# Memory output end, its norm and the first four query tiles in groups of 256 tokens

## The reference, cut to what matters

```
o = jnp.einsum('bhqm,bmhd->bqhd', p, v).reshape(bsz, seq, D_MODEL)
mem_out = o @ w_mo                                           # 1024 x 1024
x = layer_norm(DN_ALPHA * x + mem_out, ln_mem_g, ln_mem_b)   # over the 1024 channels
q = (x @ w_pq).reshape(bsz, seq, 8, 2, 128)                  # 1024 x 2048
scores = jnp.einsum('bshcd,hcnd->bshcn', q, sub_keys)
top_v, top_i = lax.top_k(scores, 16)
```

## Time and profile before

| | |
|---|---|
| median of 3 runs | 3624.01 us (3623.11 to 3626.68) |
| the profiled execution | 3621.46 us, its span 3619.7 us |
| PE, PEld busy | 3296.5 us (91%), 1950.9 us (54%) |
| DVE busy | 2804.6 us (77%) |
| ACT, POOL busy | 1479.5 us (41%), 991.1 us (27%) |
| granted TensorE clock, mean | 0.97 |

### The profile page before, as it was taken

One profiled execution on the slowest core, in us unless ns is written; L12 is line 12 of the kernel. 1 busy time (PEld: TensorE's weight loads), 2 busy tenths in 40 slices (PEclk: granted clock), 3 DMA queues, 4 the chain that ended last, 5 costly groups with the idle time before them and its releaser, 6 DMA issues. The chain is left out here.

```text
span 3619.7 us, 58425 instructions
## 1 busy us (share of the span) xinstructions
PE 3296.5 (91%) x20018; PEld 1950.9 (54%) x20018; DVE 2804.6 (77%) x5272; ACT 1479.5 (41%) x2002; POOL 991.1 (27%) x746
## 2 busy tenths in 40 slices
PE   7998979979797999999889899799797979999996
PEld 3554635646464656666445455356564646566663
DVE  6776457888888678888858763587888886888887
ACT  4334433445353543333343443333444445433333
POOL 1510100332313124444324010004223231344443
PEclk9999999999898999999999999999998989999998
DMA  5102312777878699999640032229697878999995
GB/s 176 36 1 70 117 58 97 286 285 279 302 256 324 237 391 378 378 385 370 229 147 18 1 99 88 87 82 331 245 325 256 304 276 287 391 375 384 380 368 190
DMA packets 386932, 840.93 MB, mean 232 GB/s; under 512 B 33376, under 2 KB 232032, under 8 KB 386016
## 3 DMA queue, kind: packets, MB, share of 16 engines
q1 hardware_dynamic: 312480, 565.39, 44.1%
q0 software_dynamic: 73728, 268.47, 19.7%
q10 hardware_dynamic: 576, 5.37, 0.4%
HBM read 732.14 MB, written 106.95 MB: 232 GB/s over the span
## 5 line engine op out<-in xcount | busy, mean ns | idle before, releaser
L126 PE MATMUL ps<-xh,wh 128*128 128x384 f16 (+1 forms) x2880 | 994.1, 345 | 112.2 <-DVEq L1103 47.3
L103 DVE SCALAR_TENSOR_TENSOR wl<-wf,wh 128x1024 f16<-128x1024 f32 x656 | 803.9, 1227 | 367.7 <-ACT wh L97 354.1
L97 ACT ACTIVATE wh<-wf 128x1024 f16<-128x1024 f32 x656 | 690.6, 1053 | 924.5 <-PE ps L1789 534.9
L127 PE MATMUL ps<-xl,wh 128*128 128x384 f16 (+1 forms) x2880 | 993.2, 345 | 0.0
L128 PE MATMUL ps<-xh,wl 128*128 128x384 f16 (+1 forms) x2880 | 992.7, 345 | 0.0
L1787 PE MATMUL ps<-work,wh 128*128 128x384 f16 x2048 | 668.5, 326 | 6.9 <-DVE work L2118 5.0
L1789 PE MATMUL ps<-work,wl 128*128 128x384 f16 x2048 | 668.5, 326 | 0.0
L1788 PE MATMUL ps<-work,wh 128*128 128x384 f16 x2048 | 668.5, 326 | 0.0
L1904 POOL DMA_INDIRECT xT<-urows,small x256 | 349.9, 1367 | 1062.8 <-DVE xT L1986 805.6
L1912 POOL DMA_INDIRECT work<-experts,small x256 | 440.2, 1720 | 602.1 <-DVE work L2127 592.6
L126 PEld LDWEIGHTS ps<-xh,wh 128*128 128x128 f16 x2880 | 283.8, 99 | 355.3 <-DVEq L1103 48.1
(11 more groups left out here) (384 smaller groups left out, 3999.9 us busy)
## 6 DMA issues: line engine op xcount, KB each, us to landing
wf<-experts SPq DMA_DIRECT2D x512, 512.0 KB, 5.9
wf<-proj SPq DMA_DIRECT2D x144, 512.0 KB, 3.4
gates<-work SPq DMA_DIRECT2D x96, 512.0 KB, 8.3
work<-hid SPq DMA_DIRECT2D x256, 192.0 KB, 4.5
work<-gates SPq DMA_DIRECT2D x256, 192.0 KB, 5.3
hid<-work SPq DMA_DIRECT2D x192, 192.0 KB, 6.6
hid<-small SPq DMA_DIRECT2D x64, 192.0 KB, 6.6
xsave<-xT ACTq DMA_DIRECT2D x2, 2048.0 KB, 6.5
```

Source lines behind the costliest of these rows:

```text
L97: m.nc.scalar.activation(m.wh[:, slot, :], m.wf[:, k, :], ACT.Copy, scale=WS).then_inc(m.high_done, 1)
L103: m.nc.vector.scalar_tensor_tensor(m.wl[:, slot, :], m.wf[:, k, :], WS, m.wh[:, slot, :], ALU.mult, ALU.subtract).then_inc(m.split_done, 1)
L126: m.nc.tensor.matmul(out, wh[:, k, :], xh[:, k, 0:n], start=(k == order[0]), stop=False)
L127: m.nc.tensor.matmul(out, wh[:, k, :], xl[:, k, 0:n], start=False, stop=False)
```

## The change

The tokens are cut into two halves of 256 (`half(0)`, `half(1)`), and the seam runs once for each.

- Memory output: tiles 0 to 3 stay whole. Tiles 4 to 7 are projected for half 0 first, into banks 4 to 7, then for half 1 (`late`), in the order 6, 7, 4, 5, which is that of their slots. The sum and the six variance matmuls of half 0 stand between those.
- Norm: centring and scaling take four channel blocks of 256 tokens, one fold per half, and the reciprocal, the root, the outputs and the low parts 256 tokens. VectorE does the norm of half 0, and only then that of half 1.
- Query tiles: tiles 0 and 1 go side by side, channel block by channel block, for half 0 (`projected_pair(0)`), then tile 2 for half 0, the variance of half 1, tile 3 for half 0, the pair for half 1, and tiles 2 and 3 for half 1 with the scores between. The loop starts at its second round. Tiles 0 to 3 use banks 4 to 7.
- The copy of x to memory and the first query copy wait for the low parts of both halves.

The diff, cut to its core (the helpers `half_...` do for one half what the `ln_...` helper of the same name did for all tokens):

```diff
+def half_pe_var(m, pe, n, bank_var, h, c):
+    if c == 0:
+        pe.wait_ge(n.out, 3 * h + 1)
+    else:
+        pe.wait_ge(n.sq, 2 * h + 2)
+    count = HALF_F // 2 if c == 0 else HALF_F
+    for f in range(count):
+        last = m.nc.tensor.matmul(bank_var[:, half(h)], m.ones[:, :], half_squares(m, c)[:, f, :],
+                                  start=(c == 0 and f == 0), stop=(c == 1 and f == count - 1))
+    last.then_inc(n.var, 1)
...
+def half_act_out(m, act, n, par, h, f):
+    if f == 0 and h == 0:
+        act.wait_ge(n.params, 1)
+    act.wait_ge(n.out, 3 * h + 2 + f // HALF_F)
+    x = m.xT[:, f, half(h)]
+    high = m.nc.scalar.activation(m.xh[:, f, half(h)], x, ACT.Identity, scale=m.gain[:, f:f + 1],
+                                  bias=m.bias[:, f:f + 1])
...
@@ memory: tensor @@
-        for f in range(N_MO):
+        for f in range(N_MO - RING):
...
+        for f in range(N_MO - RING, N_MO):
+            n = T_MO + f
+            wait_tile(m, pe, n // RING, n % RING)
+            project(m, B[f][:, 0:HT], n % RING, m.xh[:, :, half(0)], m.xl[:, :, half(0)], HT).then_inc(m.mo_half, 1)
+        for j, f in enumerate(MO_LATE):
+            pe.wait_ge(m.ln_mem.res_added, N_MO - RING - 1 + j if j < 2 else MO_FIRST + j - 1)
+            project(m, B[j % 2][:, 0:HT], (T_MO + f) % RING, m.xh[:, :, half(1)], m.xl[:, :, half(1)], HT)\
+                .then_inc(m.tile_used, 1)
+            if j == 0:
+                half_pe_sum(m, pe, m.ln_mem, B[2], 0, MO_FIRST)
+            if j == 2:
+                for c in range(2):
+                    half_pe_var(m, pe, m.ln_mem, B[3], 0, c)
...
-        ln_pe(m, pe, m.ln_mem, B[2], B[3])
+        half_pe_sum(m, pe, m.ln_mem, B[2], 1, MO_FIRST + RING + 1)
@@ memory: scalar @@
+        next_high(0)
+        for c in range(2):
+            half_act_square(m, act, m.ln_mem, 0, c)
+        next_high(1)
+        next_high(2)
+        half_act_sd(m, act, m.ln_mem, B[3], 0)
         for f in range(KT):
-            ln_act_out(m, act, m.ln_mem, par, f)
+            half_act_out(m, act, m.ln_mem, par, 0, f)
+        next_high(3)
+        for c in range(2):
+            half_act_square(m, act, m.ln_mem, 1, c)
+        half_act_sd(m, act, m.ln_mem, B[3], 1)
+        for f in range(KT):
+            half_act_out(m, act, m.ln_mem, par, 1, f)
@@ memory: vector @@
+        late(0)
+        split_low(m, dve, R_0, 0)
+        for c in range(2):
+            half_dve_centre(m, dve, m.ln_mem, B[2], 0, c)
+        half_dve_fold(m, dve, m.ln_mem, 0)
+        late(1)
+        split_low(m, dve, R_0, 1)
+        late(2)
         split_low(m, dve, R_0, 2)
...
+        half_dve_inverse(m, dve, m.ln_mem, step, 0)
+        half_dve_scale(m, dve, m.ln_mem, 0, 0)
+        late(3)
+        half_dve_scale(m, dve, m.ln_mem, 0, 1)
+        for i in range(KT):
+            half_dve_low(m, dve, m.ln_mem, 0, i)
+        for c in range(2):
+            half_dve_centre(m, dve, m.ln_mem, B[2], 1, c)
+        half_dve_fold(m, dve, m.ln_mem, 1)
         split_low(m, dve, R_0, 3)
...
@@ experts: tensor @@
+        def projected_pair(h):
+            for i in range(KT):
+                pe.wait_ge(m.ln_mem.low, h * KT + i + 1)
+                for k in range(2):
+                    last = project(m, B[4 + k][:, half(h)], k, m.xh[:, :, half(h)], m.xl[:, :, half(h)], HT,
+                                   LOW_ORDER, slice(i, i + 1))
+                    if h and i == KT - 1:
+                        last.then_inc(m.tile_used, 1)
...
-        with pe.Fori(0, R_PQ) as r:
+        for k in range(2):
+            wait_tile(m, pe, R_0, k)
+        projected_pair(0)
+        wait_tile(m, pe, R_0, 2)
+        projected_half(0, 2)
+        for c in range(2):
+            half_pe_var(m, pe, m.ln_mem, B[3], 1, c)
+        wait_tile(m, pe, R_0, 3)
+        projected_half(0, 3)
+        projected_pair(1)
+        score(0, 0)
+        for k in range(2, RING):
+            projected_half(1, k).then_inc(m.tile_used, 1)
+            score(0, k - 1)
+        score(0, RING - 1)
+        with pe.Fori(1, R_PQ) as r:
```

More of the change, by code:

```diff
@@ L286, in ln_dve, with half, half_pe_sum, half_squares @@
         ln_dve_low(m, dve, n, i)
+HT = SEQ // 2
+HALF_F = KT // 2
+def half(h):
+    return slice(h * HT, (h + 1) * HT)
+def half_pe_sum(m, pe, n, bank_sum, h, added):
+    pe.wait_ge(n.res_added, added)
+    m.nc.tensor.matmul(bank_sum[:, half(h)], m.ones[:, :], m.rs[:, 1, half(h)], start=True, stop=True)\
+        .then_inc(n.sum, 1)
+def half_squares(m, c):
+    return m.sq[:, c].rearrange("p a t -> p (a t)").rearrange("p (f t) -> p f t", t=HT)
+def half_pe_var(m, pe, n, bank_var, h, c):
[8 more added lines that the diff above has]
+    last.then_inc(n.var, 1)
@@ new lines, in half_pool, with half_dve_centre @@
+def half_pool(m, pool, n, par, h):
+    for i in range(KT // 2):
+        f = 2 * i
+        pool.wait_ge(n.even, h * KT // 2 + i + 1)
+        x = m.xT[:, f, half(h)]
+        m.nc.gpsimd.tensor_scalar(x, x, par[:, n.g][:, f:f + 1], par[:, n.b][:, f:f + 1], ALU.mult, ALU.add)\
+            .then_inc(n.even_out, 1)
+def half_dve_centre(m, dve, n, bank_sum, h, c):
+    if c == 0:
+        dve.wait_ge(n.sum, h + 1)
+    x = m.xT[:, c * HALF_F:(c + 1) * HALF_F, half(h)]
+    mean = bank_sum[:, half(h)].unsqueeze(1).to_broadcast([P, HALF_F, HT])
+    m.nc.vector.scalar_tensor_tensor(x, mean, -1.0 / D, x, ALU.mult, ALU.add).then_inc(n.centred, 1)
@@ L292, with half_dve_low @@
+def half_dve_low(m, dve, n, h, i):
+    f = LOW_ORDER[i]
+    if f % 2:
+        dve.wait_ge(n.odd_out, h * KT // 2 + f // 2 + 1)
+    else:
+        dve.wait_ge(n.even_out, h * KT // 2 + f // 2 + 1)
+    m.nc.vector.scalar_tensor_tensor(m.xl[:, f, half(h)], m.xT[:, f, half(h)], XS, m.xh[:, f, half(h)],
+                                     ALU.mult, ALU.subtract).then_inc(n.low, 1)
 TWO_PI = 2 * math.pi
@@ L1492, in vector, with residual, late @@
         low(XH - 1)
-        for f in range(N_MO):
+        total = m.rs[:, 1, :]
+        def residual(f, t, bank, count, last=False):
+            x = m.xT[:, f, t]
+            STT(x, bank, UNSCALE / ALPHA, x, ALU.mult, ALU.add).then_inc(m.ln_mem.res_added, 1)
+            if f == 0:
+                return
+            dve.wait_ge(m.ln_mem.res_added, count)
+            added = nc.vector.tensor_tensor(total[:, t], m.xT[:, 0, t] if f == 1 else total[:, t], x, ALU.add)
+            if last:
+                added.then_inc(m.ln_mem.res_added, 1)
+            else:
+                step(added)
+        def late(j):
+            dve.wait_ge(m.tile_used, T_PQ + j + 1)
+            residual(MO_LATE[j], half(1), B[j % 2][:, 0:HT], MO_FIRST + j + 1, last=(j == RING - 1))
+        for f in range(N_MO - RING):
             n = T_MO + f
-            if f < RING:
-                split_low(m, dve, (n + RING) // RING, n % RING)
+            split_low(m, dve, (n + RING) // RING, n % RING)
             dve.wait_ge(m.tile_used, n + 1 + RING)
-            STT(m.xT[:, f, :], B[f % 2], UNSCALE / ALPHA, m.xT[:, f, :], ALU.mult, ALU.add)\
-                .then_inc(m.ln_mem.res_added, 1)
-            ln_dve_total(m, dve, m.ln_mem, step, f)
+            residual(f, slice(0, SEQ), B[f % 2], f + 1)
+        for f in range(N_MO - RING, N_MO):
+            dve.wait_ge(m.mo_half, f - (N_MO - RING) + 1)
+            residual(f, half(0), B[f][:, 0:HT], f + 1, last=(f == N_MO - 1))
         dve.wait_ge(m.split_done, T_PQ + RING)
```

78 lines of the change are left out of this document (48 added, 30 removed).

## The result

The changed kernel ran in 3593.99 us (median of four runs, 3591.60 to 3594.75) against 3625.23 for the kernel before in the same measurement: a ratio of 0.9916, interval 0.9903 to 0.9929.

A forecast was written before the change was run, and what follows sets the result against it. TensorE, 91% busy, was taken as the bound, with 25.8 us a layer lost to the norm. A gain of 10.6 a layer, less 0.8 and 1.5, left 8.3, 16.6 in all: 3624.0 to 3607.4, range 3600 to 3616.

The forecast's parts named there:

- The timetable: Worked-out engine times from the first w_mo matmul to the second query-tile round: 81.1 us, before 91.7, so 10.6 less.
- stop ahead of the second sum: TensorE waits 3.0 us for VectorE's last late total before half 1's sum of the norm.
- stop ahead of the second pair: TensorE waits 3.1 us before query tiles 0 and 1 of half 1.
- the unshown price: VectorE's reciprocal at 256 columns, in no row: taken as 1.7 us by width, upper bound 3.35.
- The deductions: Taken off the 10.6 us a layer: 0.8 for low parts beside GpSimd and 1.5 for the clock, leaving 8.3.
- This meets both halves: 0.8: Low parts slowed beside GpSimd in both halves of the norm: 0.8 us a layer taken off.
- I take 1.5: TensorE's lower clock at the starts of both pairs after stops: 1.5 us a layer, between 0 and 2.6.
- Afterwards TensorE does not wait, so a microsecond saved here is one saved in the end: Behind the norm TensorE has no waits, so the 8.3 us a layer reach the total: 16.6 us.
- case 5: VectorE's lag or the gathers bound the expert stage and give the time back: 3624 us, chance 0.09.
- 2, the lower clock in both pairs: Lower clock stays through both pairs, 4.7 and 4.5 us more, 0.6 a layer left: about 3623, chance 0.07.
- 3: GpSimd's half-wide operations pace the low parts, at worst 2.98 us each, 11.8 more a layer: 3631, chance 0.04.
- 4: Weight loads come into the open in the 384 half matmuls, 37.6 us a layer: some 3682, chance 0.02.

The follow-up runs named there:

- a_norm_only: Changed kernel with the norm in halves but the first four query tiles whole again: 3622.52 us, ratio 1.0003 to the kernel before.
- a_one_by_one: Changed kernel with query tiles 0 and 1 one after the other in each half, not side by side: 3604.97 us.
- a_filled: Changed kernel with 96 repeated half-wide matmuls between the second pair and the first score: 3615.27 us, ratio 0.9984 to the kernel before.
- a_keep_clock: a_early_centre plus 12 and 4 small filler matmuls in TensorE's stops ahead of the second sum and the first pair: 3591.79 us.
- a_early_centre: Changed kernel with half 1's centrings between half 0's low parts, its squares earlier and its variance ahead of tile 2: 3589.64 us, ratio 0.9911 to the kernel before.
- a_gather_late: Changed kernel with two small memsets on GpSimd ahead of the first gather of expert rows in each layer: 3596.86 us.

## Why the prediction was right and wrong

**The direction and the mechanism were right.** TensorE was idle for the norm of all tokens, half tiles fill that time, and the seam is shorter by 9.6 to 9.7 us in both layers. a_norm_only shows that the filling does it, a_one_by_one that the side by side order is 4.05 of it (clock included).

**The timetable held within 1.2 us.** On the seam's clock, forecast and measured: first late addition 34.1 and 34.0; stop ahead of the second sum 3.0 and 2.97; first pair 49.1 and 49.5; stop ahead of the second pair 3.1 and 3.07; second round 81.1 before deductions and 82.1. Outputs 0.49 apart, reciprocals 1.7 (the unshown price, with bounds 1.7 and 3.35, went by width), GpSimd in time. The fold of half 1 was done at 56.9 (forecast 56.6) and TensorE came to the variance at 58.4 and not 57.3, so the chain behind it moved by 1.1, to the second pair at 66.8 (forecast 65.6). That this variance could start 2.6 us earlier, with the centrings between the low parts and tile 2 behind it, I had not seen.

**The deductions were mis-sized.** "This meets both halves: 0.8" and "I take 1.5" made 2.3 a layer; 1.0 was lost. Some 0.8 of it is the lower clock of the first pair, by the estimate above, where I had 1.5 between 0 and 2.6; the second pair lost nothing, since it ran at granted clock 1.00. What is left for low parts beside GpSimd and all else is 0.2, where I had 0.8. That is 1.3 us a layer, 2.6 of the 14.6 us missed. That the clock's part came out so small has some luck in it: in 2 of 8 seams it took 2.6 us more. And even with nothing taken off, 10.6 a layer, the working gives 3602.8 and not 3594, so the miss lies mostly elsewhere.

**The step that failed: "Afterwards TensorE does not wait, so a microsecond saved here is one saved in the end".** The second round and those behind it do run full, but in the experts' first half TensorE is idle 64 to 74 us a layer, most of it behind VectorE, whose dots wait for gathered rows (with light gathers 15 to 17 are left). I had not looked at that stretch of the trace of before. It bears on two things. The range of 16 us had no term for it, though one stretch in it takes from 631 to 644 us with the same code; a kernel whose executions lie 28 us apart can't have a range of 3600 to 3616 from a seam alone, and my reference, three runs within 3.6 us, was a sample too small to show it (102 runs have their median at 3620.8). And a gain behind the seam was in no rival: case 5 let the time only be given back.

**What is shown of the 31.2 us:** 19.3 in the seams. Larger samples bring the whole to 23.6 (standard error 2.2) on one chip, and to about 25 over all: the ten runs of the changed kernel have a mean of 3596.6, the 102 of the kernel before 3621.7. So some 6 to 8 us of the first figure were the luck of four runs. The mean of the ten is still 3.4 us below the range.

**What stays open:** the cause of the 4 to 6 us that are left. Over all traces the experts' first half took 638.5 us in 14 layers of kernels with the end of before, and 636.6 in 16 with that of after, 1.9 apart with a standard error of 1.0, which alone could be chance. The timings say more. In each of the seven later kernels built on the changed one, the mean of the runs gained more on the kernel before of its measurement than the seams explain (means of 97.7 and 88.1, or the kernel's own trace): by 0.3 to 8.1 us, 4.8 in the mean with a standard error of 1.0. For the six built on the kernel before, or equal to it, the mean gain is 0.9 with 0.8. So the rest is hardly chance. a_norm_only (2.9) and a_filled (5.4) have it too, so it needs neither the half query tiles nor a shorter seam. Nor is it the first gather's time within 0.25 us, or the written-out first round. It may be how gathers and tile loads meet in the DMA engines; no run shows it. That VectorE's program of after, pauses and all, is the cause was not tried by itself.

**The rivals.** 2, the lower clock in both pairs: in the changed kernel the clock fell for the first pair only, and it was back after 2.1 us (526.70 to 528.78); in 2 of the 8 seams with its end the second pair began at the lower level too, and they lost 2.6 us and not the 9.2 of this rival. The Trainium skill (TensorE: Matmul & The Clock Gate, HAM oscillation) says that bursts with stops between can be throttled anew each time. The trace agrees for the burst behind the stop of 2.97 us and not for the one behind 3.07, which ran at granted clock 1.00 in both layers of the changed kernel. 3 and 4 fell with GpSimd's 0.67 us and the spacing of 0.11: at 2.4 GHz TensorE started the half-wide matmuls at 527.04, 527.15 and 527.25 in a_keep_clock. 5 fell: nothing was given back.

## What to carry to other kernels

A norm between two runs of matmuls is hidden by cutting its tokens in two only if matmuls of the first half are there to stand in the second half's chain; cutting alone gave nothing (3622.5 against 3621). Next to it, look which engine the remaining stop waits for and start its chain between operations that leave it idle: the two centrings moved between the low parts, with the variance ahead of tile 2, gave another 2.4 us a layer. And before a saved microsecond is carried to the end, read the waits of every later stretch and the spread of many runs: here a stage with 70 us of waits moved the total by more than half of the effect.

## What the runs showed of the hardware

TensorE's lower clock can last longer in one layer than in the other behind the same stops. In three of the 16 seams with the end of before the last six variance records took 5.22 or 5.23 us and not 2.84; in a fourth 14 matmuls of the first query tile ran at 1.2 GHz and not 6; in 2 of 8 seams with the end of after 23 half-wide ones and not 8 or 9. After a stop of 2.97 us the next matmuls ran at 1.2 GHz. After 3.07 us, with 14 us of nearly full work ahead of it, they ran at 2.4 GHz in the other 6 of these 8. In a_one_by_one the six matmuls behind the same 3.07 us ran at 2.4 GHz, and those behind a further stop of 0.57 us at 1.2 (granted clock of the stretch 0.83). The lower clock cost 0.06 and 0.35 us where the low parts came late (a_early_centre against a_keep_clock) and 2.6 us where they did not (a_gather_late, layer one). In the changed kernel VectorE starts the maximum of the fifteenth query tile 0.48 us after ScalarE's copy has ended (626.86 to 627.34), in the kernel before 0.13 (635.66 to 635.79); its idle time there is 1.36 and 1.01 us. The first gather comes 0.35 us later in every kernel with the changed code on VectorE; eleven added operations did not bring it about in the kernel before. GpSimd's first half-wide operation took 1.82 us, the later ones 0.63 to 0.83.
